# Hybrid encoder layer: rows normalised and stored beside the last expert, its own rows completed apart

## The reference

```python
def expert_choice_ffn(h, w_router, w_gate, w_up, w_down):
    ...
    cap = EC_CAPACITY_FACTOR * T // N_EXPERTS
    aff = jax.nn.softmax((xt @ w_router).astype(F32), axis=-1)
    g, idx = lax.top_k(aff.T, cap)
    xe = xt[idx]
    he = jax.nn.silu(jnp.einsum('ecd,edf->ecf', xe, w_gate)) * jnp.einsum('ecd,edf->ecf', xe, w_up)
    ye = jnp.einsum('ecf,efd->ecd', he, w_down) * g[..., None].astype(h.dtype)
    y = jnp.zeros((T, D), h.dtype).at[idx.reshape(-1)].add(ye.reshape(-1, D))
    ...
x = x + expert_choice_ffn(rmsnorm(x, P['norm_ffn'][l]), ...)
return rmsnorm(x, norm_final)
```

## Time and profile before

| | us |
|---|---|
| median of 3 runs | 2780.35 |
| lowest, highest | 2778.39, 2784.56 |
| the profiled execution | 2778.26 |
| its span, first to last instruction | 2776.5 |
| TensorE busy | 2649.8 (95%) |
| last result on VectorE begins | 2739.68 |
| first read of all rows issued | 2747.91 |
| last tile's scale begins | 2769.92 |

### The profile page before, as it was taken

How to read it: one execution, slowest core, us unless ns; L and a number is a source line. 1 busy time by engine, 2 the same in 40 slices (tenths; PEclk the granted TensorE clock), 3 DMA queues, 4 the chain that set the end, 5 groups by cost and what they waited for, 6 DMA issues and landing times.

```text
span 2776.5 us, 29866 instructions
## 1 busy us (share of the span) xinstructions
PE 2649.8 (95%) x12410; PEld 1784.2 (64%) x12410; DVE 857.4 (31%) x1479; ACT 411.8 (15%) x935; POOL 227.6 (8%) x252
## 2 busy tenths in 40 slices
PE   7999899999989999999999999969999999999994
PEld 4554454466657777754455495538877887887783
DVE  5556732266772212144100152271111111111112
ACT  3120000244451010112100031110000000000002
POOL 0220100000010010041000000001001100100100
PEclk9999999999999999999999999979999999999997
DMA  4110211000010101221111101128877877787774
GB/s 154 31 49 23 74 46 31 1 16 1 1 46 23 45 24 31 76 106 31 46 45 30 61 31 61 73 100 300 279 250 240 267 255 261 250 280 249 240 252 161
DMA packets 189651, 314.99 MB, mean 113 GB/s; under 512 B 6027, under 2 KB 69856, under 8 KB 188929
## 3 DMA queue, kind: packets, MB, share of 16 engines
q1 hardware_dynamic: 181760, 292.74, 30.8%
q0 software_dynamic: 7808, 21.11, 3.1%
HBM read 287.61 MB, written 26.21 MB: 113 GB/s over the span
## 4 chain that ended last, share of the span: by engine, by line
PE 90%; DVE 7%; ACT 2%; issue 1%; DMA 1%; POOL 0%; DVEq 0%; ACTq 0%; SPq 0%; POOLq 0%
PE banks L692 64%; PE banks L974 9%; PE banks L873 5%; PE banks L1063 4%; PE banks L893 2%; PE banks L1269 2%; DVE arena L1732 2%; PE banks L908 1%; PE banks L708 1%; PE banks L1238 1%; DVE arena L1589 1%; DVE arena L2086 0%; DVE arena L2089 0%; ACT arena L1550 0%; DVE arena L2084 0%
## 5 line engine op out<-in xcount | busy, mean ns | idle before, releaser
L692 PE MATMUL banks<-arena 128*128 128x160 f32 (+3 forms) x8388 | 1896.2, 387 | 24.0 <-ACT arena L1328 8.0
L692 PEld LDWEIGHTS banks<-arena 128*128 128x128 f32 x8388 | 1306.0, 191 | 607.1 <-issue 548.9
L974 PE MATMUL banks<-arena 128*128 128x320 f32 x896 | 243.5, 433 | 2.6 <-DVE arena L1868 2.1
L974 PEld LDWEIGHTS banks<-arena 128*128 128x128 f32 x896 | 169.7, 190 | 72.5 <-issue 2.3
L2156 DVE TENSOR_TENSOR arena<-arena,banks 128x160 f32<-128x160 f32 x128 | 41.1, 321 | 521.3 <-ACT arena L1539 521.3
L1539 ACT ACTIVATE arena<-banks 128x160 f32<-128x160 f32 x128 | 38.9, 304 | 824.7 <-PE banks L692 824.7
L606 POOL TENSOR_TENSOR arena<-arena 128x512 f32<-128x512 f32 (+1 forms) x56 | 87.0, 1567 | 876.5 <-DMA arena<-in_w_br_hyena 750.0
L873 PE MATMUL banks<-arena 128*128 128x512 f32 (+1 forms) x384 | 142.7, 522 | 2.5 <-DVE arena L1772 2.5
L1063 PE MATMUL banks<-arena 128*128 128x512 f32 x280 | 122.6, 593 | 0.7 <-ACT arena L1468 0.7
L1832 DVE TENSOR_REDUCE att<-banks 128x1 f32<-128x1024 f32 (+1 forms) x80 | 81.3, 1058 | 125.5 <-PE banks L893 125.4
L873 PEld LDWEIGHTS banks<-arena 128*128 128x128 f32 x384 | 70.5, 190 | 55.4 <-issue 52.4
(11 more groups left out here) (207 smaller groups left out, 1450.9 us busy)
## 6 DMA issues: line engine op xcount, KB each, us to landing
arena<-in_w_exp_gate SPq DMA_DIRECT2D x32, 2048.0 KB, 8.0
arena<-in_w_exp_up SPq DMA_DIRECT2D x32, 2048.0 KB, 12.9
arena<-in_w_exp_down SPq DMA_DIRECT2D x32, 2048.0 KB, 18.4
arena<-in_w_in SPq DMA_DIRECT2D x36, 512.0 KB, 4.0
arena<-in_x_prompt SPq DMA_DIRECT2D x8, 1024.0 KB, 7.9
residual_rows<-arena SPq DMA_DIRECT2D x10, 512.0 KB, 2.6
normed_rows<-arena SPq DMA_DIRECT2D x10, 512.0 KB, 2.6
arena<-residual_rows SPq DMA_DIRECT2D x5, 1024.0 KB, 9.1
```

Source lines behind the costliest of these rows:

```text
L692: last = pe.matmul(out, l, r, start=(n == 0), stop=(n == len(pairs) - 1))
L974: last = pe.matmul(PS[:, 3 * (g % 2) + bank, 0:GN], l[:, k, :], r[:, k, :], start=(k == 0 and which in (G1, G2, G5)), stop=(k == 3), skip_ ...
```

## The change

SyncE does not wait for the last expert's scatters any more. As soon as expert 14's have landed it reads all rows, into places of the arena that are free by then. ScalarE's silus of the last expert leave the loop, and squares of the first six tiles stand between and behind the last three of them; the other four follow, then one root for all ten tiles. VectorE scales the ten tiles, and SyncE stores them, without the last expert's share in them.

GpSimd gathers the last expert's own rows a second time, now from `acc`, into `LASTP` and `LASTQ`. TensorE computes the last expert's sample rows ahead of its prompt rows. VectorE adds the gated results to the gathered rows in SBUF, ScalarE sums their squares (those of the sample rows by quarters, of which TensorE sums four with the matrix `SAMEROW`), and the finished rows are stored by two plain scatters to the outputs, over what the ten stores wrote there; GpSimd waits for all ten before that. A gain laid out by quarters (`GQ`) and the row numbers of the quarters in the sample output (`last_q`, one more copy in the routing) are new.

```diff
+        last_q = small("last_q", [P, 1], U32)
...
-        FIN = [at(4 * t, D) for t in range(NT)]
+        FIN_AT = [64, 72, 80, 88, 166]
+        FIN = [at(FIN_AT[t // 2] + 4 * (t % 2), D) for t in range(NT)]
+        LASTP, LASTQ, GQ, SAMEROW = at(174, D), at(178, 256), at(179, 256), at(180, P)
+        LSUM = at(181, 8)
...
-            sp.wait_ge(sem["gu_mm"], 8 * NE)
-            sp.wait_ge(sem["scatter_p"], 16 * NE)
-            sp.wait_ge(sem["scatter_s"], 16 * NE)
-            for t in range(0, NT, 2):
-                sp.dma_start(at(4 * t, 2, D), acc[t * P:(t + 2) * P, :].rearrange("(t p) d -> p t d", p=P)).then_inc(sem[f"fin_in_{t // 2}"], 16)
+            for j in range(4):
+                sp.dma_start(GQ[CS * j:CS * (j + 1), :], a["norm_final"][256 * j:256 * (j + 1)].unsqueeze(0).to_broadcast([CS, 256])
+                             ).then_inc(sem["gain_in"], 16)
+            sp.wait_ge(sem["scatter_p"], 16 * (NE - 1))
+            sp.wait_ge(sem["scatter_s"], 16 * (NE - 1))
+            for i in range(NT // 2):
+                sp.dma_start(at(FIN_AT[i], 2, D), acc[2 * i * P:2 * (i + 1) * P, :].rearrange("(t p) d -> p t d", p=P)
+                             ).then_inc(sem[f"fin_in_{i}"], 16)
             for t in range(NT):
                 sp.wait_ge(sem["fin_ready"], t + 1)
                 sp.dma_start(out_rows[t], FIN[t]).then_inc(sem["fin_out"], 16)
             sp.wait_ge(sem["fin_out"], 16 * NT)
+            sp.wait_ge(sem["scatter_p"], 16 * NE)
+            sp.wait_ge(sem["scatter_s"], 16 * NE)
...
-                    pool.wait_ge(sem["idx_ready"], 5)
+                    pool.wait_ge(sem["idx_ready"], 6)
...
-            scatter(NE - 1, False)
+
+            last = NE - 1
+            pool.wait_ge(sem["scatter_p"], last * 16)
+            pool.wait_ge(sem["scatter_s"], last * 16)
+            pool.tensor_copy(out_p_idx[:, :], idx_p[:, last:NE]).then_inc(sem["scol_ready"], 1)
+            pool.tensor_copy(out_q_idx[:, :], idx_q[:, last:NE]).then_inc(sem["scol_ready"], 1)
+            pool.wait_ge(sem["scol_ready"], last * 2 + 2)
+            pool.tensor_tensor(turn[:, :], ones[:, 0:1], ones[:, 0:1], ALU.mult)
+            pool.indirect_dma_start(LASTP, None, acc, bass.IndirectOffsetOnAxis(ap=out_p_idx[:, 0:1], axis=0)).then_inc(sem["gather_p"], 16)
+            pool.indirect_dma_start(LASTQ, None, acc_quarters, bass.IndirectOffsetOnAxis(ap=out_q_idx[:, 0:1], axis=0)).then_inc(sem["gather_s"], 16)
+            pool.wait_ge(sem["fin_out"], 16 * NT)
+            pool.wait_ge(sem["y_out"], last * 3 + 1)
+            pool.indirect_dma_start(out_s[0].rearrange("t (j n) -> (t j) n", j=4), bass.IndirectOffsetOnAxis(ap=last_q[:, 0:1], axis=0),
+                                    YS, None).then_inc(sem["scatter_s"], 16)
+            pool.wait_ge(sem["y_out"], last * 3 + 3)
+            pool.indirect_dma_start(out_p[0], bass.IndirectOffsetOnAxis(ap=out_p_idx[:, 0:1], axis=0), YP, None).then_inc(sem["scatter_p"], 16)
...
-            down(NE - 1, False, True)
+            wait("he_ready", NE * 8)
+            wait("y_out", NE * 3 - 3)
+            wait("ed0", NE * 16)
+            wait("ed1", NE * 16)
+            down_sample()
+            down_prompt(NE - 1, False)
+            wait("fin_act", NT + 2)
+            product(PS[:, 0, 0:1], [(SAMEROW, LSUM[:, 0:1])]).then_inc(sem["norm_mm"], 1)
...
-            with act.Fori(1, NE) as e:
+            with act.Fori(1, NE - 1) as e:
                 silus(e, False)
 
             fin = Count(act, sem["fin_act"])
-            for t in range(NT):
+
+            def fin_square(t):
                 act.wait_ge(sem[f"fin_in_{t // 2}"], 16)
                 if t:
                     fin.wait()
                 fin.inc(act.activation(SQJ, FIN[t], ACT.Square, accum_out=stat[:, 0, t:t + 1]))
-                fin.wait()
-                fin.inc(act.activation(stat[:, 1, t:t + 1], stat[:, 0, t:t + 1], ACT.Sqrt, scale=1.0 / D, bias=eps[:, 0:1]))
+
+            for f in range(FF // P):
+                act.wait_ge(sem["gu_mm"], (NE - 1) * 8 + f + 1)
+                act.wait_ge(sem["he_ready"], (NE - 1) * 8 + f - 1)
+                act.activation(SL[:, f % 2, :], PS[:, f % 3, 0:CE], ACT.Silu).then_inc(sem["silu_ready"], 1)
+                if f >= 5:
+                    fin_square(2 * f - 10)
+                    fin_square(2 * f - 9)
+            for t in range(6, NT):
+                fin_square(t)
+            fin.wait()
+            fin.inc(act.activation(stat[:, 1, 0:NT], stat[:, 0, 0:NT], ACT.Sqrt, scale=1.0 / D, bias=eps[:, 0:1]))
+            act.wait_ge(sem["fin_rec"], 1)
+            fin.inc(act.activation(SQJ[:, 0:256], YS, ACT.Square, accum_out=LSUM[:, 0:1]))
+            act.wait_ge(sem["fin_rec"], 2)
+            fin.wait()
+            fin.inc(act.activation(SQJ[:, 0:512], YP[:, 0:512], ACT.Square, accum_out=LSUM[:, 1:2]))
+            act.wait_ge(sem["norm_mm"], 2)
+            fin.inc(act.activation(LSUM[:, 3:4], PS[:, 0, 0:1], ACT.Sqrt, scale=1.0 / D, bias=eps[:, 0:1]))
+            act.wait_ge(sem["fin_rec"], 3)
+            fin.wait()
+            fin.inc(act.activation(SQJ[:, 512:1024], YP[:, 512:1024], ACT.Square, accum_out=LSUM[:, 2:3]))
+            act.wait_ge(sem["fin_rec"], 4)
+            fin.inc(act.activation(LSUM[:, 5:6], LSUM[:, 4:5], ACT.Sqrt, scale=1.0 / D, bias=eps[:, 0:1]))
...
+            dve.tensor_scalar(last_q[:, :], PS[:, 4, 2 * NE - 1:2 * NE], float(-4 * LP), None, ALU.add).then_inc(sem["idx_ready"], 1)
...
-            results(NE - 1, False)
-
-            dve.wait_ge(sem["gain_in"], 16)
-            for t in range(NT):
-                dve.wait_ge(sem["fin_act"], 2 * t + 2)
-                step.inc(dve.reciprocal(stat[:, 2, t:t + 1], stat[:, 1, t:t + 1]))
-                step.wait()
+
+            for j in range(4):
+                if j:
+                    step.wait()
+                src = ident[:, CS * j:CS * (j + 1)]
+                step.inc(dve.tensor_copy(SAMEROW[:, 0:CS], src) if j == 0 else
+                         dve.tensor_tensor(SAMEROW[:, 0:CS], SAMEROW[:, 0:CS], src, ALU.add))
+            step.wait()
+            for j in range(1, 4):
+                step.inc(dve.tensor_copy(SAMEROW[:, CS * j:CS * (j + 1)], SAMEROW[:, 0:CS]))
+            step.wait()
+
+            def fin_scaled(t):
                 dve.scalar_tensor_tensor(FIN[t], FIN[t], stat[:, 2, t:t + 1], GROW, ALU.mult, ALU.mult).then_inc(sem["fin_ready"], 1)
+
+            def last_added(dst, bank, gate, row):
+                dve.scalar_tensor_tensor(dst, bank, gate, row, ALU.mult, ALU.add).then_inc(sem["fin_rec"], 1)
+
+            last = NE - 1
+            dve.wait_ge(sem["gain_in"], 80)
+            dve.wait_ge(sem["fin_act"], NT + 1)
+            step.inc(dve.reciprocal(stat[:, 2, 0:NT], stat[:, 1, 0:NT]))
+            step.wait()
+            dve.wait_ge(sem["scatter_p"], last * 16)
+            dve.wait_ge(sem["scatter_s"], last * 16)
+            dve.wait_ge(sem["gather_p"], 16 * NE + 16)
+            dve.wait_ge(sem["gather_s"], 16 * NE + 16)
+            fin_scaled(0)
+            dve.wait_ge(sem["dn_mm"], last * 3 + 1)
+            last_added(YS, PS[:, 5, 0:256], gates[:, 1, last:NE], LASTQ)
+            for t in range(1, 6):
+                fin_scaled(t)
+            dve.wait_ge(sem["dn_mm"], last * 3 + 2)
+            last_added(YP[:, 0:512], PS[:, 6, :], gates[:, 0, last:NE], LASTP[:, 0:512])
+            for t in range(6, NT):
+                fin_scaled(t)
+            dve.wait_ge(sem["fin_act"], NT + 4)
+            step.inc(dve.reciprocal(LSUM[:, 6:7], LSUM[:, 3:4]))
+            step.wait()
+            dve.scalar_tensor_tensor(YS, YS, LSUM[:, 6:7], GQ, ALU.mult, ALU.mult).then_inc(sem["y_out"], 1)
+            dve.wait_ge(sem["dn_mm"], last * 3 + 3)
+            last_added(YP[:, 512:1024], PS[:, 7, :], gates[:, 0, last:NE], LASTP[:, 512:1024])
+            dve.wait_ge(sem["fin_act"], NT + 5)
+            dve.tensor_tensor(LSUM[:, 4:5], LSUM[:, 1:2], LSUM[:, 2:3], ALU.add).then_inc(sem["fin_rec"], 1)
+            dve.wait_ge(sem["fin_act"], NT + 6)
+            step.inc(dve.reciprocal(LSUM[:, 7:8], LSUM[:, 5:6]))
+            step.wait()
+            for n in range(2):
+                cols = slice(n * 512, (n + 1) * 512)
+                dve.scalar_tensor_tensor(YP[:, cols], YP[:, cols], LSUM[:, 7:8], GROW[:, cols], ALU.mult, ALU.mult).then_inc(sem["y_out"], 1)
```

More of the change, by code:

```diff
@@ L147 @@
 gu_mm silu_ready he_ready scol_ready dn_mm y_out scatter_p scatter_s gain_in
-fin_act fin_ready fin_out""".split() + [f"fin_in_{t}" for t in range(NT // 2)]
+fin_act fin_rec fin_ready fin_out""".split() + [f"fin_in_{t}" for t in range(NT // 2)]
 def encoder_kernel(nc, a, out_p, out_s):
@@ L1230, in turn_slots @@
                 if first:
-                    wait("idx_ready", 5)
+                    wait("idx_ready", 6)
                 wait("gather_p", e * 16 + 16)
@@ L1255, in gate_up, with down_prompt @@
                     last.then_inc(sem["gu_mm"], 1)
```

(24 more changed lines are left out.)

## The result

The changed kernel takes 2760.08 us (median of 5 runs, 2757.71 to 2767.76) against 2780.27 for the kernel before; the ratio is 0.9934, with a 95% interval of 0.9921 to 0.9947. That is some 20 us less where 22 were forecast, inside the range.

A forecast was written before the change was run, and what follows sets the result against it. The prediction saw the old kernel limited by a 36.85 us tail without TensorE work, VectorE becoming the new bound; its terms summed to span 2753.8, 22.7 less, giving 2758 us, range for 8 in 10 2754 to 2767.

The forecast's parts named there:

- forecast clock: A time in the changed kernel's first profile less 9.80 us, for comparison with the forecast's times.
- 5 us of cover or more: Early reads beside the last expert: they land at least 5 us before ScalarE's squares want them.
- Squares, root, table: ScalarE around the last silus: six squares follow the last silu, one table load 1.28, root 0.29, ending at 2730.4.
- The last rows: Completing the last expert's rows after VectorE's block ends at 2744.0: 4.5 us, ready at 2748.5.
- Stores: SyncE's ten tile stores: last issued at 2744.0, lands 2.6 us later, at 2746.6.
- The rival that they pile up: Tile stores take 7.7 us to land, delaying GpSimd's prompt scatter to 2753.7; 2763 in all; chance 0.14.
- GpSimd beside VectorE: Rival at the sample scatter: VectorE's last halves delay its issue, prompt scatter 1.7 later, 2759.4 in all; chance 0.06.
- I take the gather: Final prompt scatter: 4.4 us from issue to landing, as for a plain gather of as many bytes.
- 0.5 to the end of the span: End of the program: 0.5 us from the prompt scatter's landing at 2753.2 to the span's end at 2753.7.
- forecast tail of 31.7: Expected time from the last expert's first down product to the end of the span: 31.7 us.
- the end within 6 us: Sign in the timeline: GpSimd's last two DMAs at 2747 to 2749 and the end within 6 us.
- The slower rival: Late reads hold ScalarE's seventh silu, delaying down products; slower if landing beyond 2741, some 2790 at 2751; chance 0.03.

The follow-up runs named there:

- squares_after: Changed kernel with all ten squares behind the last silu: tail 38.63 us (changed 33.69), median 2766.26 us, ratio 0.9940 to the kernel before.
- squares_early: Changed kernel with squares starting one silu earlier, four instead of six behind the last: tail 31.16 us, median 2758.24 us, ratio 0.9920 to before.
- reads_late: Changed kernel with the five reads waiting for the last down product and all squares behind the last silu: tail 62.04 us, median 2788.97 us, ratio 1.0029.
- gain_ahead: Changed kernel with early squares, eight tiles multiplied by the gain before the root, and sample rows first: tail 29.48 us, median 2755.97 us, ratio 0.9910.
- the second measurement: Changed kernel run again without any edit: tail 33.66 us, median 2757.70 us, ratio 0.9919 to the kernel before.
- stored_by_sync: Changed kernel with the last expert's finished rows stored by two plain SyncE stores instead of GpSimd's scatters: tail 29.18 us, median 2755.60 us, ratio 0.9909.

## Why the prediction was right, and where it was not

**The bound.** Right. The forecast had VectorE as the new bound, 4.3 us behind TensorE; VectorE's block ends at 2743.94 on the forecast clock (2744.0 forecast), TensorE 4.3 us earlier. squares_after and squares_early move the end by what they move the squares.

**Reads.** Issued at 2698.64 on the forecast clock (2698.8). But the step that gave them "5 us of cover or more" was too generous, and one thing was not seen at all. One of the four small gain loads held SyncE for 7.07 us, so that it came to its wait for the scatters only 2.5 us ahead of them; the forecast said of these loads only that nothing waits for them, and left out that they stand ahead of the reads on SyncE. And the first read landed 10.8 us after its issue, at 2709.5, where the rates gave 2707.9; squares_early, which asks for it 4.35 us sooner, waits for it. The 1.6 us are about what the two gathers' 0.64 MB take at 415 GB/s (an estimate: 1.5 us), which the forecast had put behind the first read: they were issued after that read and landed before it, at 2718.1 and 2718.9 against 2719.2 in the profile. In reads_late, with neither gathers nor weights beside it, the first read lands in 4.8 us. No run parts gathers from weights. The cover was 3.4 us, enough for the changed kernel.

**Squares, root, table.** Right. Six squares took 7.35 us (7.1 forecast), the root ended at 2730.46 (2730.4), the first scale started at 2730.84 (2730.7). No silu needed a table load between squares, and the root followed its load by 0.02 us. The drain of 1380 ns that the Trainium skill, page "ScalarE: Activation LUTs", section "What ACT_TABLE_LOAD costs", adds to a switch is not in this trace either.

**The last rows.** Ready at 2748.12 (2748.5). The overlap of VectorE's neighbours was of the size taken from the earlier trace rows: five scales in a row take 6.06 us.

**Stores.** Right. The last one landed in 2.93 us (2.6). The rival that they pile up did not come: their median is 2.8 us, where the first of before took 7.7 behind the reads. In gain_ahead, where they come faster, it does: the median is 5.0 us and they decide the end.

**GpSimd beside VectorE.** The sample scatter's issue took 1.17 us beside VectorE's two halves, and 1.01 in gain_ahead, where it ran while VectorE was idle. The Trainium skill, page "SBUF — State Buffer", section "Who interferes with whom", has a VectorE instruction with two SBUF inputs contend with a GpSimd instruction that reads SBUF. If that is what shows here, which no run settles, it is worth 0.16 us, against the 1.7 that the rival charged.

**The scatter and the end.** This is where the sum was off. The term "I take the gather", 4.4 us, was 1.1 too high: the plain scatter lands in 3.3, between the plain store and the gather. The term "0.5 to the end of the span" was 3.25 too low: 3.75 us from the last landing to the end. It was taken from a tail in which SyncE's stores came last, and carried over to one in which GpSimd's scatters do. With 0.15 gained ahead of the scatter, which starts at 2748.65 on the forecast clock (2748.8), that makes 2.0, the difference between the forecast tail of 31.7 and the measured 33.69. The two errors partly cancel, so the sum looks better than its terms. The sign "the end within 6 us" of GpSimd's last DMAs failed: it came 7.05 us after the start of the last one. And that the second measurement's median, 2757.70, meets the forecast of 2758 almost exactly is luck, since executions arrive at the last expert up to 10 us apart. Before, GpSimd's drain could have been read in the trace, with its end at 2750.7, 2.8 us behind the issue of the reads that waits for the last scatter's landing, but off the chain.

**The slower rival.** Its place was right in so far as late reads do turn the change into a loss: reads_late, with the reads at TensorE's end, is 7.6 us slower in the tail. It is not the mechanism that the rival named, though: there late reads hold up silus and TensorE, here they stand behind both. The edge between, where reads hold up single silus, was not tried.

## What to carry to other kernels

A tail that runs behind the last matmul is worth moving beside it, if the little that depends on that matmul can be kept apart and patched in; but look at what the rearranged tail costs by itself, since here it is slower than the old one without the overlap. When the engine that issues the last DMA changes, take the time from the last landing to the program's end from a place where that engine's DMA was last, not from the old end. With executions that reach the place of the change 10 us apart, measure from a landmark shortly ahead of it.

## What the runs showed of the hardware

GpSimd's closing drain lasts until some 3 us after its own last DMA has landed: it ended 5.8 us after the end of the last issue in the changed kernel (7265 ns from 2758.0), 3.3 us behind SyncE's drain, and in stored_by_sync it ran 12.0 us behind gathers, hidden. From the landing of its last DMA to the drain's end are 3.5 us in the changed kernel and 2.9 both before and in stored_by_sync. What it waits for stays open.

The granted TensorE clock in the stretch from 200 to 600 us was 0.96 in one execution and 0.99 in another with the same program, and the last expert started 9.57 us apart. It is not that stretch alone: in gain_ahead, where it has 0.99 too, the last expert started at 2726.72. What made the clock differ stays open.

A load of 32 KB that repeats a row over partitions, issued behind two loads of 2 MB, kept SyncE busy for 7.07 us where its neighbours took 0.42 (issues of the four gain loads in the changed kernel; duration ns min/median/max, first and last start):

```profile
L572 SPq DMA_DIRECT2D arena<-in_norm_final x4: 421/424/7073, 2697.4 to 2705.4; - x4
```

In the other runs the four issues take 8.1 to 8.5 us together, as here (8.48). Whether the loads ahead of it or its own form made it wait was not tried.
